# Prompt attention: the odd group's probabilities are scaled on GpSimd, the even group's on VectorE

## The reference

```python
p_c = masked_softmax(jnp.einsum('bqgrd,bjgd->bgrqj', qg, cmp_kv[:, :, 0]), ...)
o_c = jnp.einsum('bgrqj,bjgd->bqgrd', p_c, cmp_kv[:, :, 1])
...
o = g[..., 0:1] * o_c + g[..., 1:2] * o_s + g[..., 2:3] * o_w
```

## Time and profile before

| | us |
|---|---|
| median of 3 runs (2232.35 to 2234.95) | 2232.92 |
| the profiled execution | 2232.96 |
| its span | 2231.3 |
| TensorE busy (share of the span) | 2003.6 (90%) |
| VectorE busy | 811.1 (36%) |
| ScalarE busy | 656.8 (29%) |
| GpSimd busy | 127.8 (6%) |

### The profile page before, as it was taken

How to read it: one execution, slowest core, us unless ns; L and a number is a source line. 1 busy time by engine, 2 the same in 40 slices (tenths; PEclk the granted TensorE clock), 3 DMA queues, 4 the chain that set the end, 5 groups by cost and what they waited for, 6 DMA issues and landing times. The chain is left out here.

```text
span 2231.3 us, 35777 instructions
## 1 busy us (share of the span) xinstructions
PE 2003.6 (90%) x13239; PEld 1450.1 (65%) x13239; DVE 811.1 (36%) x1898; ACT 656.8 (29%) x1446; POOL 127.8 (6%) x260
## 2 busy tenths in 40 slices
PE   5999978984999899999999999799986799996986
PEld 3775445442344755556777776699964799995764
DVE  2001144344021066753444444211125545554344
ACT  2112000121000267653434443211113355552232
POOL 0000000000000000002111110000002011110002
PEclk8999989995999589999999999799998799997998
DMA  8452111462520020005666653222231123321221
GB/s 295 166 183 95 38 44 39 150 227 94 160 95 32 13 80 2 1 27 184 190 194 201 196 182 106 67 76 76 77 117 58 39 81 88 94 77 47 67 76 68
DMA packets 189091, 228.63 MB, mean 102 GB/s; under 512 B 21591, under 2 KB 142364, under 8 KB 188691
## 3 DMA queue, kind: packets, MB, share of 16 engines
q1 hardware_dynamic: 180030, 197.88, 27.8%
q0 software_dynamic: 8960, 29.37, 4.2%
HBM read 211.68 MB, written 23.85 MB: 106 GB/s over the span
## 5 line engine op out<-in xcount | busy, mean ns | idle before, releaser
L199 PE MATMUL ps<-h_high,up_split_weights 128*128 128x272 f32 x1408 | 235.8, 290 | 6.5 <-DVE h_low L187 6.5
L199 PEld LDWEIGHTS ps<-h_high,up_split_weights 128*128 128x128 f32 x1408 | 199.7, 190 | 6.6 <-issue 6.6
L237 PE MATMUL ps<-weights,h_fm 128*128 128x512 f32 (+1 forms) x400 | 175.0, 598 | 9.5 <-DMA rope_table<-in_rope 9.5
L2341 PE MATMUL ps<-ffn_out_split_weights,ffn_out_split_lhs 128*128 128x512 f32 (+1 forms) x660 | 157.2, 401 | 5.6 <-DVE ffn_out_y L2397 5.6
L1462 PE MATMUL ps<-dc_segments_fm,cmp_w_sb 64*128 64x128 f32 x2048 | 147.1, 283 | 0.2 <-DVE dc_segments_fm L1501 0.2
L2341 PEld LDWEIGHTS ps<-ffn_out_split_weights,ffn_out_split_lhs 128*128 128x128 f32 (+1 forms) x660 | 116.3, 177 | 47.5 <-issue 7.6
L199 PE MATMUL ps<-h_low,up_split_weights 128*128 128x272 f32 x704 | 145.9, 289 | 0.0
L237 PEld LDWEIGHTS ps<-weights,h_fm 128*128 128x128 f32 (+1 forms) x400 | 69.4, 176 | 114.3 <-issue 104.7
L1462 PEld LDWEIGHTS ps<-dc_segments_fm,cmp_w_sb 64*128 64x128 f32 x2048 | 124.7, 187 | 21.0 <-issue 21.0
L1582 POOL DMA_DIRECT2D weights<-in_cache_cmp_kv x112 | 60.4, 539 | 1263.6 <-issue 1263.6
L598 PE MATMUL ps<-h_fm,weights 128*128 128x272 f32 x512 | 124.0, 402 | 1.6 <-ACTq L653 1.6
(11 more groups left out here) (448 smaller groups left out, 3080.9 us busy)
## 6 DMA issues: line engine op xcount, KB each, us to landing
slc_pages<-in_cache_slc_kv SPq DMA_DIRECT2D x256, 128.0 KB, 2.2
weights<-in_cache_cmp_kv POOLq DMA_DIRECT2D x112, 256.0 KB, 3.7
weights<-in_w_in SPq DMA_DIRECT2D x13, 2048.0 KB, 7.8
weights<-in_w_up SPq DMA_DIRECT2D x44, 512.0 KB, 4.6
ada_rest_weights<-in_w_ada SPq DMA_DIRECT2D x16, 1024.0 KB, 7.4
weights<-in_w_down SPq DMA_DIRECT2D x10, 1024.0 KB, 5.1
mlstm_fm_then_residual<-in_state_C SPq DMA_DIRECT2D x8, 1024.0 KB, 6.2
out_s_C<-c_new SPq DMA_DIRECT2D x8, 1024.0 KB, 8.6
```

The lines of the kernel that those rows point to most:

```text
L199: last = pe.matmul(out(half), a[:, k, c0:c0 + P], b[:, k, half * HALF:(half + 1) * HALF], start=k == 0 and n == 0, stop=k == KT - 1 and n ...
L237: last = pe.matmul(ps[0:rows(t), (at + t) % 5, 0:width], lhs[:, k, cols(t)], w[:, k, c0:c0 + width], start=k == 0, stop=k == ktiles - 1)
L2341: last = pe.matmul(s.ps[0:rows(t), t, :], x[:, k, cols(t)], w[:, k, :], start=k0 + k == 0 and term == 0, stop=k0 + k == ktiles - 1 and ter ...
```

## The change

The loop over the two halves goes out of `scale` on VectorE, which keeps o = 0. A program for GpSimd is added to the block. It goes through the 96 units and multiplies the half o = 1. Before the first unit of each tile it waits for the new semaphore `a_gated`, which VectorE raises when `alpha` of the tile is written. Each of its scales raises `a_odd_scaled`, for which TensorE waits ahead of the transposes of the odd half. From the third tile on VectorE waits, ahead of the product with the gates, for the scales on GpSimd of the tile that used the same place of `alpha`.

```diff
@@ -1605,6 +1605,7 @@
+        gated, scaled_odd = sem("a_gated"), sem("a_odd_scaled")
@@ -1656,7 +1657,7 @@
             def turn(n):

                 for o in range(2):
-                    pe.wait_ge(scaled, 2 * n + o + 1)
+                    pe.wait_ge(scaled_odd if o else scaled, n + 1)
@@ -1746,13 +1747,15 @@
                 gate = s.branch_gates[:, i, :].rearrange("q (p o h x) -> q p o h x", p=2, o=2, h=R)[:, p, :, r, :]
+                if t >= 2:
+                    dve.wait_ge(scaled_odd, 3 * t - 3)
                 link(dve.tensor_tensor(alpha[:, k], alpha[:, k], gate, ALU.mult))
+                dve.sem_inc(gated, 1)

             def scale(n):
                 br, k = UNITS[n][3], n // 3 % 2
-                for o in range(2):
-                    out = held(n, o)[:, 0:keys(n)]
-                    dve.tensor_scalar(out, out, alpha[:, k, o, br:br + 1], None, ALU.mult).then_inc(scaled, 1)
+                out = held(n, 0)[:, 0:keys(n)]
+                dve.tensor_scalar(out, out, alpha[:, k, 0, br:br + 1], None, ALU.mult).then_inc(scaled, 1)
@@ -1772,6 +1775,16 @@
+        @block.gpsimd
+        def _(pool):
+
+            for n in range(N):
+                if n % 3 == 0:
+                    pool.wait_ge(gated, n // 3 + 1)
+                br, k = UNITS[n][3], n // 3 % 2
+                out = held(n, 1)[:, 0:keys(n)]
+                pool.tensor_scalar(out, out, alpha[:, k, 1, br:br + 1], None, ALU.mult).then_inc(scaled_odd, 1)
```

## The result

The changed kernel takes 2226.54 us, the kernel before 2233.74 us (medians of 19 runs each): a ratio of 0.9965, with a 95% interval of 0.995 to 0.9981. The forecast was 2232.4 us and no difference.

The account below looks back on a forecast made before the run. TensorE was taken to bound prompt attention. Per pass -0.15 + 0.08 = -0.07 us, for seven passes -0.5 us, gave 2232.9 - 0.5 = 2232.4 us; range 2229.0 to 2238.0.

Parts of the forecast that it names:

- Which engine bounds the stage: Prompt attention: TensorE sets the pace, busy 185.5 of 197 us; VectorE, busy 133.8, does not.
- Removed from VectorE, -0.15 us a pass: 96 odd-half scales leave VectorE; only one 31-column scale ahead of finish() counts, 0.15 us a pass.
- hole A: TensorE's 0.72 us idle time around finish(), ending at 846.70 in one pass, where VectorE is late.
- The step on the 256-column scales: Just after finish(): removing these scales gives nothing more, since ScalarE's next exponent stands right behind its own move.
- Added to VectorE, 0.08: Per tile, a semaphore release and an already fulfilled wait for GpSimd, 0.04 us each; bounds 0 to 0.16.
- Added on GpSimd: 96 scales on the idle GpSimd, at most 2.6 us per tile against 6.3 available, so covered.
- rival 1: 384-column tile: GpSimd slow enough to hold up VectorE, above 1.45 us a scale; 2240 us at 5 ns a column; chance 0.06.
- hole B: TensorE's 0.42 us idle time ending at 855.12; the 512-column maxima waited for scores, so not VectorE's doing.
- Rival 3: First use of the new operation on GpSimd costs several us once, time near 2238; chance 0.03.
- The two engines against each other: GpSimd's and VectorE's scales take one port pair in turn; VectorE's 512-column scale waits, without holding up TensorE.
- Rival 2, the clock: Changed holes alter how many passes run at lowered TensorE clock, 1.55 us each; chance 0.05 slower, 0.10 faster.
- shorter ones removed the two: Shorter holes remove both lowered-clock passes seen in the profile before: 2229.3 us; chance 0.10.

Follow-up runs that it names:

- the odd half left out: Against the kernel before: VectorE scales only the even half, nobody scales the odd half, GpSimd has no program; ratio 0.9977, median 2224.87 us.
- the kernel with GpSimd beside: Against the kernel before: VectorE scales both halves, GpSimd does 96 scales of the same widths on its own buffer, nobody waits; ratio 1.0022, median 2235.43 us.

## Why the prediction was wrong

*Which engine bounds the stage*: right. VectorE's waiting for scores grew from 60.5 to 72.8 us (I said about 85), and TensorE waits for GpSimd nowhere.

*Removed from VectorE, -0.15 us a pass*: about 0.20. With the odd half left out a pass is 0.30 us shorter. 0.15 lies ahead of finish(), as forecast (hole A 0.57 instead of 0.72). The step on the 256-column scales, "give nothing more", failed: the two sets of transposes there start 1.54 us apart (840.69 and 842.23), against 1.59 before (846.70 and 848.29), and 1.52 in the changed kernel (837.60 and 839.12). That is 0.05 or a little more. The other 0.1 us doesn't look like VectorE's. In two units of the pass TensorE takes 0.56 and 0.77 us from the first transpose to the next scores instead of 0.62 and 0.83; between the even and the odd transposes there stood the wait that this kernel leaves out. The changed kernel keeps it and takes 0.60 and 0.83.

*Added to VectorE, 0.08*: 0.11, all of it the release. Above the value taken, within the bound of 0.16. The sum of both, -0.07 a pass, came near the measured -0.10 by luck, because one error stood against another: hole A gave 0.04 and not 0.07, and the rest came from behind it, where nothing was expected.

*Added on GpSimd*: the bound from above, 2.3 ns a column, was none. With one input it takes 2.8 ns a column (0.597 us for 128 columns, 1.655 for 512); how much of that is waiting for VectorE no run shows. The cover still held: rival 1 needed over 1.45 us for 384 columns, and they take 1.24; hole B is 0.42 us as before. Rival 3 didn't come either: GpSimd's first three scales, of 31 and twice 128 columns, took 1.57 us together (at 777.79), no more than 0.41 and twice 0.60.

*The two engines against each other*: right. The assumption that the one-input scale takes part is borne out: in the changed kernel, GpSimd works from 846.49 on, and VectorE's 512-column scale at 847.87 takes 0.83 us, not 0.48, with no consequence for the maxima at 849.24:

```profile
846.49 3.64 POOL L1787 TENSOR_SCALAR prob<-prob,alpha 128x31 f32<-128x31 f32 x3 [3.94 <-DVEq L1753]
...
847.87 0.83 DVE L1758 TENSOR_SCALAR prob<-prob,alpha 128x512 f32<-128x512 f32 x1
849.24 0.49 DVE L1735 TENSOR_REDUCE minus_max<-ps 128x1 f32<-128x128 f32 x2 [0.55 <-PE ps L1655]
```

By what the Trainium skill says of the shared port pair ("SBUF — State Buffer", "SBUF: two separate sides"), a one-input fp32 scale in two-port mode and a GpSimd instruction exclude each other; this row and the 0.641 us of the kernel with GpSimd beside agree.

*Rival 2, the clock, is where it went wrong.* I had the mechanism, its place and its price (1.55 us a lowering; 1.5 measured), and the case "shorter ones removed the two". I gave that case 0.10 and at most 3.1 us, because the holes change by a small part of themselves, and so treated the count as about proportional to the hole. The measured count isn't: the four profiles of before have 13 lowerings in 28 stretches, the four of the changed kernel 3 in 28, and over all runs of the table the mean clock is 0.9291 against 0.9261. A lowering depends on a hole's place in time as well as on its length (above), and the change moves both: the hole by 0.04 us, and every later hole by another 0.1 us a pass. The step had two further faults. I read two lowerings from the one profile of before and missed the third, in the tail (at 978.0 us; the last stretch takes 20.75 us against 19.2 at full clock). And I took one profile's count for the kernel's. The sign that I had named for this step, a change in the number of passes with a lowered clock, is the one that came.

What is shown and what isn't: with hole A gone there is no lowering (none in 14 stretches, with GpSimd or without), and with longer holes there are more (5, 5 and 6 of 7). How much of the fall from 13 to 3 is the hole's length, how much the place of the holes, and how much four profiles by chance, isn't separated. No run kept the holes' length and moved only their place.

The sum as the runs give it: before minus after, means of the table, is 6.0 us (2232.3 - 2226.3). At a common clock 1.2 us of it remain, uncertain by 0.4, where seven passes of 0.10 are 0.7. The four profiled stages of each kernel, from the first score to the next block's first VectorE instruction, took 213.4, 217.7, 217.7 and 211.8 us before, and 211.8, 208.1, 208.1 and 211.0 after: 215.2 and 209.8 on the average, 5.4 us. Of these, 2.5 lowerings fewer (13/4 - 3/4) at 1.5 us are 3.8, the passes 0.7; the rest, about 0.9 us, is how long the clock stays low at the stage's beginning, which I take for chance: 13 to 23 us of it lie in the stage, in either kernel (on the average 19.4 before, 17.0 after). What is left of the 7.2 us between the medians I take for chance ahead of and behind the stage; no run shows it. That the count of lowerings is really 0.75 against 3.25 rests on four profiles each.

That a busier or less busy TensorE moves its clock is also what the Trainium skill says ("TensorE: Matmul & The Clock Gate", "Part 1: The HAM clock gate"). The counts here agree in that. By that, a hole matters beyond its own length; here the change was worth 0.1 us a pass by itself and some 0.5 us by the clock (3.8 us in seven stretches).

## What to carry to other kernels

Where TensorE is nearly saturated, look for the holes that recur, and ask of each two prices: its length, and the chance that the clock is lowered behind it. The second isn't in proportion to the first, and it changes with the hole's place in time, so a tenth of a microsecond can come with several times itself, either way. Take the number of lowerings from several profiles before forecasting, and compare kernels at a common mean clock. And look for what makes the hole: moving two copies by a few instructions gave at least as much as the second engine did, and with them moved the second engine gave nothing (2223.8 and 2223.5 us).

## What the runs showed of the hardware that I had not expected

- TensorE idle for 0.68 to 1.42 us, once in a pass of 25 us, can be followed by a lowering of its clock (33 cases, 1.6 to 2.6 us behind the hole, 1.5 us each). Whether it is depends on the hole's length (0 of 14 stretches where it is 0.41 us, 6 of 6 at 0.96) and on its place in time (behind 0.72 us in 6 of 16, and not behind one of 1.31).
- The same instructions ahead of the stage took from 772.9 to 785.2 us to reach its first score, with 133.8 to 168.4 us at 1.2 GHz.
- A one-input multiplication on GpSimd takes 0.41, 0.60, 0.92, 1.24 and 1.66 us for 31, 128, 256, 384 and 512 columns, beside a VectorE that works too; VectorE alone takes 0.24 to 0.48.
- A semaphore release that stands as an instruction of its own on VectorE cost 0.11 to 0.12 us (two kernels); a wait that was already fulfilled cost nothing visible (0.04 us between two instructions with it and without).
